# One product for each mean, after additions on VectorE: layer norms of a convolution and of four retention heads

## What is computed

```python
c   = conv(u, conv_w) + conv_b                        # depthwise, width 31, D_CONV = 1024
mu  = mean(c, -1); var = mean((c - mu)**2, -1)         # over the 1024 features
cn  = (c - mu) * rsqrt(var + EPS) * ln_g + ln_b
y_a = silu(cn) @ w_conv_out
o, S_new = retention(q, k, v, S)                       # 4 heads, RET_DV = 512
omu = mean(o, -1); ovar = mean((o - omu)**2, -1)       # over the 512 features of each head
y_b = (((o - omu) * rsqrt(ovar + EPS)) * gn_g * silu(g_ret)) @ w_ret_out
x  += (sigmoid(gA) * y_a + sigmoid(gB) * y_b) @ w_o
x  += hierarchical_moe(rmsnorm(x))                     # 16 experts, two of them per token
```

## Time and profile before

| | |
|---|---|
| median of 3 runs | 817.04 us (814.58 to 817.72) |
| profiled execution | 814.54 us |
| its span, first to last instruction | 812.60 us |
| mean granted TensorE clock | 0.986 |
| busy: TensorE, VectorE, ScalarE, POOL | 780.3, 660.8, 508.2, 96.9 us |
| chain that ended last | TensorE 87%, VectorE 8%, ScalarE 2% |

### The profile page before, as it was taken

The page is one execution under the profiler, slowest core; times in us unless marked ns, Lnnn a source line. Parts: engine busy times, 40 slices in busy tenths (PEclk is TensorE's granted clock), DMA queues, the critical chain, the costliest instruction groups (busy, mean ns, idle before and its releaser), DMA issues.

```text
span 812.6 us, 12152 instructions
## 1 busy us (share of the span) xinstructions
PE 780.3 (96%) x4781; PEld 665.1 (82%) x4781; DVE 660.8 (81%) x885; ACT 508.2 (63%) x632; POOL 96.9 (12%) x120
## 2 busy tenths in 40 slices
PE   8989999999999999999889897999999999999994
PEld 4989999767676699999789894788888888888873
DVE  5698999767687878899567567789899889989987
ACT  7324446566667675435384362688888888888873
POOL 0100000233243200000002001011111121110000
PEclk9999999999999999999999998999999999999998
DMA  9944454688888736455248544699999999999972
GB/s 336 384 159 169 161 192 157 241 322 314 273 291 268 298 128 215 156 178 186 104 136 317 209 169 161 222 343 377 381 378 367 362 368 356 378 375 353 356 276 83
DMA packets 39173, 213.27 MB, mean 262 GB/s; under 512 B 7381, under 2 KB 7637, under 8 KB 19244
## 3 DMA queue, kind: packets, MB, share of 16 engines
q1 hardware_dynamic: 23268, 165.39, 55.0%
q0 software_dynamic: 15408, 45.71, 16.2%
q10 hardware_dynamic: 432, 1.31, 0.4%
HBM read 193.45 MB, written 31.65 MB: 277 GB/s over the span
## 4 chain that ended last, share of the span: by engine, by line
PE 87%; DVE 8%; ACT 2%; issue 1%; DMA 1%; DVEq 0%; ACTq 0%
PE bank L1559 36%; PE bank L1837 32%; PE bank L1671 3%; PE bank L1706 2%; PE bank L1617 2%; DVE w_lo L1086 2%; DVE conv L1122 2%; PE bank L1827 2%; PE bank L1721 1%; PE bank L1735 1%; PE bank L1742 1%; PE bank L1682 1%; PE bank L1585 1%; PE bank L1867 1%; PE bank L1755 1%
## 5 line engine op out<-in xcount | busy, mean ns | idle before, releaser
L1559 PE MATMUL bank<-h_hi,w_hi 128*128 128x264 f32 (+1 forms) x640 | 189.2, 296 | 5.1 <-DVE w_lo L1086 5.0
L1559 PE MATMUL bank<-h_lo,w_hi 128*128 128x264 f32 (+1 forms) x640 | 184.5, 288 | 0.0
L1559 PE MATMUL bank<-h_hi,w_lo 128*128 128x264 f32 (+1 forms) x640 | 184.4, 288 | 0.0
L1091 DVE TENSOR_TENSOR ring_lo<-raw,ring_hi 128x2048 fp32r<-128x2048 f32 x72 | 163.6, 2289 | 25.3 <-ACT ring_hi L762 25.3
L1086 DVE TENSOR_TENSOR w_lo<-raw,w_hi 128x1024 fp32r<-128x1024 f32 x112 | 136.8, 1223 | 42.3 <-ACT w_hi L755 42.0
L755 ACT ACTIVATE w_hi<-raw 128x1024 fp32r<-128x1024 f32 x112 | 117.9, 1052 | 74.2 <-PE bank L1559 73.8
L762 ACT ACTIVATE ring_hi<-raw 128x2048 fp32r<-128x2048 f32 x72 | 138.2, 1920 | 19.3 <-PE bank L1837 19.3
L1559 PEld LDWEIGHTS bank<-h_hi,w_hi 128*128 128x128 f32 x640 | 120.9, 189 | 10.3 <-DVE w_lo L1086 7.1
L1559 PEld LDWEIGHTS bank<-h_lo,w_hi 128*128 128x128 f32 x640 | 120.9, 189 | 0.6 <-issue 0.2
L1559 PEld LDWEIGHTS bank<-h_hi,w_lo 128*128 128x128 f32 x640 | 120.8, 189 | 0.0
L1122 DVE SCALAR_TENSOR_TENSOR conv<-u,vec,conv 128x256 f32<-128x256 f32 x240 | 101.8, 480 | 0.2
(11 more groups left out here) (280 smaller groups left out, 1488.9 us busy)
## 6 DMA issues: line engine op xcount, KB each, us to landing
raw<-weights SPq DMA_DIRECT2D x152, 1024.0 KB, 7.2
S_ring<-in_state_ret POOLq DMA_DIRECT2D x26, 512.0 KB, 6.7
out_ret_sample<-S_ring POOLq DMA_DIRECT2D x26, 512.0 KB, 6.4
S_five<-in_state_ret POOLq DMA_DIRECT2D x6, 512.0 KB, 4.7
out_ret_sample<-S_five POOLq DMA_DIRECT2D x6, 512.0 KB, 7.3
out_ret_prompt<-S_out POOLq DMA_DIRECT2D x8, 256.0 KB, 4.8
y_rows<-xg POOLq DMA_DIRECT2D x4, 512.0 KB, 6.8
raw<-y_rows SPq DMA_DIRECT2D x2, 1024.0 KB, 6.1
```

The costliest lines, as they stand in the source:

```text
L1091: dve.tensor_tensor(ring_view(ring_lo, k), raw[raw_slot(NCM + k)][:, :].rearrange("p (k n) -> p k n", k=4), ring_view(ring_hi, k).bitcast( ...
L1559: ins = pe.matmul(out, a[:, k, cols], b[:, k0 + k, :], start=first and k == 0 and j == 0, stop=last and k == ks - 1 and j == 2)
```

## The change

Means: VectorE first adds the blocks in halves (8 to 4 to 2 to 1, or 4 to 2 to 1), and TensorE multiplies the one sum. This is done for `lm`, `lv`, `gm` and `gv`. The first of the sums of a head stands at k = 4h + 6 on VectorE, behind the step's other work, `gm` with subtraction and square at k = 4h + 7, the sum of the squares at k = 4h + 8, `gv` with root, reciprocal and product at k = 4h + 9. The tile list moves with it. Of the convolution, the first sum stands at the end of unit 85 on VectorE, the second in unit 88. The second `turn_over(2)` before the first expert is gone, and VectorE's `lo_chunk(2)` stands behind the first expert's `x_lo` instead of in front.

```diff
+            def halved(dst, src, n):
+                while n > 1:
+                    n //= 2
+                    ins = dve.tensor_tensor(dst[:, 0:n, OUT], src[:, 0:n, OUT], src[:, n:2 * n, OUT], ALU.add)
+                    src = dst
+                    if n > 1:
+                        link(ins)
+                return ins
...
# VectorE, behind the step's block
+                    if k >= 6 and (k - 6) % 4 == 0 and k <= 18:
+                        h = (k - 6) // 4
+                        evacuated(dve, ("ot", h))
+                        halved(gsq, oT[:, 4 * h:4 * h + 4, :], 4).then_inc(gsum_ready, 1)
+                    if k >= 8 and k % 4 == 0 and k <= 20:
+                        h = (k - 8) // 4
+                        dve.wait_ge(osq_ready, h + 1)
+                        halved(gsq, gsq, 4).then_inc(gsum_ready, 1)
                 conv_steps(conv_quota(w))
                 if w == LN_MEAN - 1:
...
                     last.then_inc(conv_step, 1)
+                    all_stored(dve)
+                    dve.wait_ge(conv_step, KT * CW + 1)
+                    halved(ln_sq, conv, KT).then_inc(csum_ready, 1)
...
                 if w == LN_VAR:
+                    dve.wait_ge(csq_ready, 1)
+                    halved(ln_sq, ln_sq, KT).then_inc(csum_ready, 1)
                     evacuated(dve, ("lv",))
                     link(dve.reciprocal(rstd[:, OUT], rstd[:, OUT]))
                     rb = rstd[:, OUT].rearrange("p (a t) -> p a t", a=1).broadcast_to([128, KT, N])
-                    dve.wait_ge(csq_ready, 1)
...
# TensorE
-                    if k >= 6 and (k - 6) % 4 == 0 and k <= 18:
-                        h = (k - 6) // 4
-                        evacuated(pe, ("ot", h))
-                        b = opened(("gm", h))
-                        for et in range(4):
-                            ins = pe.matmul(b[:, OUT], cst("mean_v"), oT[:, 4 * h + et, OUT], start=et == 0, stop=et == 3)
-                        done(ins)
                     if k >= 7 and (k - 7) % 4 == 0 and k <= 19:
                         h = (k - 7) // 4
-                        pe.wait_ge(osq_ready, h + 1)
+                        pe.wait_ge(gsum_ready, 2 * h + 1)
+                        b = opened(("gm", h))
+                        done(pe.matmul(b[:, OUT], cst("mean_v"), gsq[:, 0, OUT], start=True, stop=True))
+                    if k >= 9 and (k - 9) % 4 == 0 and k <= 21:
+                        h = (k - 9) // 4
+                        pe.wait_ge(gsum_ready, 2 * h + 2)
                         b = opened(("gv", h))
-                        for et in range(4):
-                            ins = pe.matmul(b[:, OUT], cst("mean_v"), gsq[:, et, OUT], start=et == 0, stop=et == 3)
-                        done(ins)
+                        done(pe.matmul(b[:, OUT], cst("mean_v"), gsq[:, 0, OUT], start=True, stop=True))
...
                 if w == LN_MEAN:
-                    pe.wait_ge(conv_step, KT * CW + 1)
+                    pe.wait_ge(csum_ready, 1)
...
                 if w == LN_VAR:
-                    pe.wait_ge(csq_ready, 1)
+                    pe.wait_ge(csum_ready, 2)
...
                 if not rd:
                     last_places()
-                    turn_over(2)
                 to_features(0, rd)
...
# VectorE, before and in the experts
-            lo_chunk(2)
...
                 x_parts(0, rd)
+                if rd == 0:
+                    lo_chunk(2)
```

More of the change, by code:

```diff
@@ L255, in _tiles @@
                 add((("ot", (k - 5) // 4), "A"))
-            if k >= 6 and (k - 6) % 4 == 0 and k <= 18:
-                add((("gm", (k - 6) // 4), "D"))
             if k >= 7 and (k - 7) % 4 == 0 and k <= 19:
-                add((("gv", (k - 7) // 4), "A"))
+                add((("gm", (k - 7) // 4), "D"))
+            if k >= 9 and (k - 9) % 4 == 0 and k <= 21:
+                add((("gv", (k - 9) // 4), "A"))
             if k in (20, 21):
@@ L920, in _ @@
                                             bank(("ot", h))[:, 0:32].rearrange("p (f n) -> p f n", f=4), ACT.Copy))
-                    if k >= 6 and (k - 6) % 4 == 0 and k <= 18:
-                        h = (k - 6) // 4
[L923 to L926, removed]
                     if k >= 7 and (k - 7) % 4 == 0 and k <= 19:
                         h = (k - 7) // 4
+                        evacuated(act, ("gm", h))
+                        act.activation(gsq[:, :, OUT], oT[:, 4 * h:4 * h + 4, OUT], ACT.Square).then_inc(osq_ready, 1)
+                    if k >= 9 and (k - 9) % 4 == 0 and k <= 21:
+                        h = (k - 9) // 4
                         seen(act, ("gv", h))
@@ L1263, in _ @@
                             free(ins)
-                    if k >= 6 and (k - 6) % 4 == 0 and k <= 18:
-                        h = (k - 6) // 4
+                    if k >= 7 and (k - 7) % 4 == 0 and k <= 19:
+                        h = (k - 7) // 4
                         seen(dve, ("gm", h))
@@ L1270, in _ @@
                         free(dve.tensor_tensor(v, v, mb, ALU.subtract))
-                    if k >= 7 and (k - 7) % 4 == 0 and k <= 19:
-                        h = (k - 7) // 4
+                    if k >= 9 and (k - 9) % 4 == 0 and k <= 21:
+                        h = (k - 9) // 4
                         evacuated(dve, ("gv", h))
@@ L1279, in _ @@
                         dve.wait_ge(std_ready, h + 1)
+                if STEP0 <= w < STEP0 + STEPS:
+                    k = w - STEP0
+                    if k >= 6 and (k - 6) % 4 == 0 and k <= 18:
[6 more added lines that the diff above has]
+                        halved(gsq, gsq, 4).then_inc(gsum_ready, 1)
                 conv_steps(conv_quota(w))
@@ L1751, in _ @@
                 if w == LN_MEAN:
-                    pe.wait_ge(conv_step, KT * CW + 1)
+                    pe.wait_ge(csum_ready, 1)
                     b = opened(("lm",))
-                    for f in range(KT):
-                        ins = pe.matmul(b[:, OUT], cst("mean_d"), conv[:, f, OUT], start=f == 0, stop=f == KT - 1)
-                    done(ins)
+                    done(pe.matmul(b[:, OUT], cst("mean_d"), ln_sq[:, 0, OUT], start=True, stop=True))
                 if w == LN_VAR:
-                    pe.wait_ge(csq_ready, 1)
+                    pe.wait_ge(csum_ready, 2)
                     b = opened(("lv",))
-                    for f in range(KT):
-                        ins = pe.matmul(b[:, OUT], cst("mean_d"), ln_sq[:, f, OUT], start=f == 0, stop=f == KT - 1)
-                    done(ins)
+                    done(pe.matmul(b[:, OUT], cst("mean_d"), ln_sq[:, 0, OUT], start=True, stop=True))
             evacuated(pe, ("m", NMIX - 2))
```

2 lines of the change are left out of this document (1 added, 1 removed).

## The result

The changed kernel takes 817.01 us (median of 20 runs, 812.90 to 821.54), the kernel before in the same job 814.82 us (20 runs, 810.36 to 819.66). The ratio is 1.0034, 95% interval 1.0018 to 1.0050: 2.8 us slower (1.5 to 4.1). The profiled executions are 818.06 us (span 816.25) and 814.54 us (span 812.60), 3.65 us of span apart. The forecast was -0.6 us.

What follows compares the result with a forecast made beforehand. TensorE was taken as the bound, 87% of the span in the chain of waits. Heads -0.2, convolution's norm +2.1 and experts' start -2.5 sum to -0.6 us, 816.4 us on the 817.04 median; 8-in-10 range 808 to 822.

Steps and rivals of the forecast that it cites:

- Part 2: Convolution's norm: second sum held in VectorE's queue, half clock behind the variance wait; +2.1 us, other bound +0.4.
- products 89 and 90 lose half of a like stretch, 1.7 us: Behind the convolution's variance wait TensorE's clock falls to half, so these products take 1.7 us longer.
- The fall at the mean costs nothing: Convolution's norm: low clock behind the mean's wait costs 0, as units 87 and 88 have time before the variance.
- the 7.6 us of products bring nothing: Convolution's norm: TensorE passes saved gain nothing, since the stretch's end hangs on the variance and what follows it.
- the one for the norm: Sign of being wrong: last convolution steps to first `cout` product (39.7 us) changes by more than 3 us.
- The clock term: Half clock behind the new wait at the convolution's variance, 1.7 us; nothing counted for `cout` to `pt`.
- Part 1: Heads' norms: 11.2 us off TensorE, of which waits take back 10.9; -0.2 us.
- far from 11: Sign of being wrong: TensorE's idle time between units 41 and 64, in the heads, far from 11 us.
- Part 3: Experts' start: unread products dropped, `lo_chunk(2)` later and hidden, first expert product earlier; -2.5 us, between -2.9 and -1.2.
- The heads' gain stays: Heads: TensorE never waits, so -11.2 us stays and the kernel takes 803.3 us; chance 0.10 in full, 0.15 in part.
- The state transfers as a pace setter: Heads: state loads and stores slow down on busy DMA, heads +4.3 us, kernel 822.2 us; chance 0.18.
- The third rival: Heads and convolution: sums no cheaper than products replaced, or no effect; only experts' start counts, -2.5, 814.5 us; chance 0.12.

Runs made afterwards that it cites:

- e2: Only the convolution's norm changed, heads and experts' start as in the kernel before: 817.39 us, 1.0036 of the kernel before.
- f2: Convolution's norm and experts' start changed, heads as in the kernel before: 815.40 us, 1.0005 of the kernel before.
- h3: The changed kernel timed once more, in another job: 816.13 us, 1.0017 of the kernel before.
- f1: The changed kernel without the sums of the convolution's norm, so heads and experts' start alone: 810.95 us, 0.9961 of the kernel before.
- h1: The kernel before with only the mean's sum of the convolution's norm added: 814.82 us, 1.0015 of the kernel before.
- g3: The changed kernel with the second sum of the convolution's norm one unit earlier in VectorE's program: 814.81 us, 0.9993 of the kernel before.
- e3: Only the experts' start changed, heads and norm as in the kernel before: 812.20 us, 0.9973 of the kernel before.
- g2: Heads and experts' start changed, plus only the variance's sum of the convolution's norm: 817.28 us, 1.0035 of the kernel before.
- h2: The kernel before with only the variance's sum of the convolution's norm added: 817.90 us, 1.0049 of the kernel before.
- e1: Only the heads' norms changed, convolution and experts as in the kernel before: 814.90 us, 1.0012 of the kernel before.
- h4: Heads and experts' start changed, plus three unread products before the wait for head 3's first sum: 811.93 us, 0.9963 of the kernel before.
- e4: Only the convolution's norm changed, plus six and five unread products in TensorE's two waits there: 816.80 us, 1.0032 of the kernel before.
- f3: The changed kernel plus unread products in the norm's two waits (six, three) and head 3's first-sum wait (three): 816.68 us, 1.0010 of the kernel before.
- f4: Only the experts' start changed, plus six unread products before the wait for the last convolution step: 813.10 us, 0.9979 of the kernel before.
- g4: Heads and experts' start changed, plus three unread products before the wait for the last convolution step: 811.74 us, 0.9956 of the kernel before.
- g1: Heads and experts' start changed, plus only the mean's sum of the convolution's norm: 813.75 us, 0.9988 of the kernel before.

## Why the prediction was wrong, point by point

**Part 2, the norm, and the clock behind it: the step that failed, by its size.** Queue and wait were right. With the 0.47 us taken off by which this execution was late at the convolution, the second sum ran from 401.7 to 404.2 (forecast 401.9 to 404.35) and the variance was there at 405.49 (forecast 404.9 to 405.3); TensorE's wait was 3.33 (forecast 3.3 to 3.8). That is +0.74 us by the queue (forecast +0.4). The step that failed is "products 89 and 90 lose half of a like stretch, 1.7 us", with nothing for the clock further on. In the profile of the first job the products took 8.09 in place of 5.85 us, +2.24, since the stretch at half clock was twice as long: +2.98 in all against +2.1. In the profiles of e2, f2 and h3 the stretch was the 3.4 us of the forecast, the Silus came 1.7 to 1.8 us later than before, and up to there +2.1 was a fair forecast. What it left out lies behind: the clock fell once more, behind the Silus in h3 (+1.57 us) and between `cout` and `pt` in the first job (+1.48), and both stretches had 0 in the sum. By ratios the norm costs 0.36% alone (e2), 2.9 us (0.9 to 4.9), and +2.1 lies within that. On top of heads and experts' start (changed kernel against f1) it is 6 us (3.4 to 8.4) by the first job and 4.6 (1.8 to 7.3) by h3.

"The fall at the mean costs nothing" held (h1 in its profile: +0.2 us), and "the 7.6 us of products bring nothing" held too. g3 confirms the cause by moving it: the sum 1.15 us earlier, no half clock behind the variance, 3.9 us earlier at the Silu. Of the two signs of being wrong, the one for the norm was only just reached: last convolution steps to first `cout` product changed by 3.02 us in the first job, 3.33 in h3.

The rule of the Trainium skill that I cited ("TensorE: Matmul & The Clock Gate", section "Loop structure matters more than you think") pointed the right way: the waits of 5.52, 3.33 and 3.2 us of the changed kernel were all followed by 1.2 GHz. It does not hold each time: the wait of 2.9 us for the last convolution step was followed by half clock in before, e3, f1, g2 and h2, and not in e1 and h4 (clock 1.00 up to 396 us). Nor is it in the rule how much follows, and that was my error: I took one length, 3.4 us, from one row.

**The clock term was only counted where TensorE waits anew.** The forecast left `cout` to `pt` at 0; in the first job it is +1.48, and one stretch at half clock there is 6.8 us long in place of 3.4; in h3 it is +0.22. The end is +0.83 in both. Over all runs the changed kernel spends 44.4 us at half clock, before 26.0. Within the runs of one kernel, time rises with this figure by 0.21 to 0.44 us per us (one fit for each of the kernels). At 0.4, taken from before, 18.4 us more are 7.4 us, and without them the changed kernel would be 4.6 us faster, not 2.8 slower; at the 0.31 and 0.21 of the changed kernel's own runs it would be 2.9 or 1.1 us faster. This is arithmetic, not an experiment. Where I tried to take the half clock away with idle products (e4, f3, f4, g4, h4), the ratio moved by -0.04, -0.24 (-0.07 against h3), +0.06, -0.05 and +0.02% from the same kernel without them, all within the intervals: either they cost what they gave, or the clock fell elsewhere. So that half clock costs time in a stretch is shown (8.09 against 5.84 us for the same products in g3); that the total of it explains the total of the time is not.

**Part 1, the heads: -0.2 forecast, +0.47 in the profile.** By ratios +0.12% alone (e1) and -0.12% on top of e3 (f1 / e3, 0.9961 / 0.9973), so nothing that can be told. The mechanism held in two places: 3.2 us before head 3's mean (forecast 3.2), 1.9 at `samp_o` of step 14 (forecast 2.9). At head 3's variance (forecast 1.9) TensorE did not wait, at the other places 0.5 us at most. Nor did it hold in its sum: I had set 10.9 us of waits, and "far from 11" as the sign of being wrong. TensorE is idle 6.9 us from 162.1 us to unit 64 (0.2 before), its busy time fell by 6.1 in place of 11.2, and 1.7 of the difference is half clock. Some 3.4 us I can't place; ends of products are modelled in the trace, and some are missing from it. What I did not see at all is that a heads' wait can be followed by half clock or not. The nine profiled experiments with the heads' sums all have the same 1.87 us of idle time in this window (1.88 in three of them), 1.6 of it in one wait for a state update; columns as before. e1:

```profile
242.00:278.00 36.00, 34.12 (x202) 22.78 (x201) 30.56 (x51) 22.99 (x36) 11.85 (x17) 1.00 0.83 289
```

and g1:

```profile
242.00:278.00 36.00, 34.13 (x195) 23.80 (x195) 30.57 (x50) 22.78 (x37) 11.81 (x17) 0.91 0.85 293
```

Same idle time, clock 1.00 in six of them and in the changed kernel (idle 2.0 us there), 0.91 in three (g1, g2, g3), and unit 64 starts at 317.8 to 320.0 us in the first, at 322.0 to 323.6 in the others. The code up to there is the same in f1 and g1. So the heads cost about nothing or +2.5 to +4 us from one execution to the next. Kernels without the heads' sums never showed it in seven profiles (unit 64 at 318.2 to 319.9). The Trainium skill says of the clock ("TensorE: Matmul & The Clock Gate", section "Part 1: The HAM clock gate (the "warmup" mystery)") that the number of slow matmuls at a kernel's start varies from run to run of the same kernel. These ten executions show such a variation in mid-kernel: 7 without and 3 with a stretch at half clock behind the same wait.

**Part 3: -2.5 forecast, -2.15 in the profile, -0.27% (2.2 us) alone.** Right in mechanism and size. In the changed kernel the clock was at half from 506.4 to 516.6, in e3 only from 507.0 to 510.4, and e3 needs 4.00 us from `pt` to the first expert product and the changed kernel 5.02. The forecast left the rest of the kernel at 0. In every profile with this part it is longer than before, by 0.4 to 0.95 us, in those without it by 0.0 to 0.4: some of the +0.83 may therefore be this part's; if all of it is, part 3 nets 1.3 us in the profile of the first job and 2.4 in h3.

**The rivals.** "The heads' gain stays" is out, and with it the rule of the Trainium skill ("Perfetto Trace Analysis", section "Identifying the Most-Contended Engine"), as I had applied it: TensorE at 96% of the span was relieved of 7.1 us and the kernel lost 2.8. That section of the Trainium skill itself calls matmul occupancy a poor measure for TensorE and names the share of the weight loads in its place. That share is 82% before, beside VectorE's 81%, so by this measure the rule does not single out TensorE. The state transfers as a pace setter are not seen: TensorE's idle time from 162.1 to 278 us is 3.0 us. The third rival, norms of no effect, is out by e2 and h2.

**Left open.** The three parts alone add to about +0.2% (1.0012, 1.0036 and 0.9973 multiplied: 1.0021), the changed kernel has 1.0034 and 1.0017; so a sum of the parts is not excluded. But by pairs, the norm costs 0.32 to 0.36% without the heads' sums and 0.56 to 0.73% with them, a difference that the intervals (0.25 to 0.4% each way) do not settle. The half clock goes the same way: 8 to 9 us more by the norm without the heads' sums (34.3 - 26, 35.5 - 26.1), 13 to 17 us with them (39.8 and 44.4 - 27.0). How an earlier wait could make a later one dearer, no run shows.

## What to carry to other kernels

Before you put additions on another engine in front of a product, look at what stands ahead of them in that engine's queue at that moment, not at its busy share: the mean's sum followed its input directly and was nearly free, the variance's sum started 3.7 us after its input was there, behind two weights' `lo`, one of which waited for its own input, and carried the loss. One place further ahead in the queue (g3) took the loss away (0.9993 of the kernel before). A wait of TensorE costs itself and, in some executions, nearly as much again in half clock, there or further on: a forecast that adds such a wait needs a range for the clock, not one length from one row. Don't count on unread products, which lowered the time at half clock in four of five kernels here and moved no ratio beyond its interval. Take a change apart before you drop it: heads and experts' start without the norm's sums (f1) are 0.4% faster than the kernel before, and most of that, 0.27%, is the experts' start.

## What was unexpected of the hardware

- The same wait of 1.6 us in the same piece of program, seen in the nine experiments with the heads' sums, was followed by 2.4 GHz in six and by 6.8 us at 1.2 GHz in three. A wait of 2.9 us for the last convolution step was followed by 1.2 GHz in five kernels and not in two.
- Stretches at half clock came as 3.4, 6.8, 10.2 or 20.5 us. Taken away at one place they turned up later: behind the Silus (418.2 to 421.6 in g4, none in f1) or over the whole routing (20.5 us in e4).
- One and the same kernel differs by 8 to 11 us between executions of one job (f1: 808.0 to 816.4, before: 808.8 to 819.9), mostly along with its time at half clock (correlation 0.66 to 0.97): a single profile tells little of a change of 3 us.
